# The fourth part of a modulation's weighted sums, moved from before the first latent head to beside it

## What is computed

```python
sh_m, sc_m, gt_m, sh_f, sc_f, gt_f = jnp.split(jax.nn.silu(c) @ w_ada + b_ada, 6, axis=-1)
h_lat = x * (1.0 + sc_m) + sh_m
q, k, v, log_decay_fwd, log_decay_bwd, g, p, bg = split(h_lat @ w_in)      # 4 heads
o = gla(q, k, v, log_decay_fwd, s_fwd) + flip(gla(flip(q), ...))           # chunks of 64 tokens
y = (sigmoid(bg_gla) * gla_output(o, g) + sigmoid(bg_pool) * pool(p)) @ w_out
x = layer_norm(ALPHA * x + gt_m * y)
x = layer_norm(ALPHA * x + gt_f * swiglu(x * (1.0 + sc_f) + sh_f))
```

## Time and profile before

| | us |
|---|---|
| median of three executions | 3194.3 |
| lowest, highest | 3191.63, 3194.87 |
| the profiled execution: its own time | 3199.43 |
| the profiled execution: span of the trace | 3197.8 |
| TensorE busy | 3015.1 (94%) |
| VectorE busy | 2197.3 (69%) |
| ScalarE busy | 1458.5 (46%) |

### The profile page before, as it was taken

The page is one execution under the profiler, slowest core; times in us unless marked ns, Lnnn a source line. Parts: engine busy times, 40 slices in busy tenths (PEclk is TensorE's granted clock), DMA queues, the critical chain, the costliest instruction groups (busy, mean ns, idle before and its releaser), DMA issues.

```text
span 3197.8 us, 40247 instructions
## 1 busy us (share of the span) xinstructions
PE 3015.1 (94%) x16596; PEld 2565.2 (80%) x16596; DVE 2197.3 (69%) x2696; ACT 1458.5 (46%) x1927; POOL 8.5 (0%) x21
## 2 busy tenths in 40 slices
PE   8989898999999999989949999999998999999997
PEld 7877787888888888866837787888876888888886
DVE  6455766899898977655566666658867776555556
ACT  5434655544444445444413444544443444444444
POOL 0000000000000000000000000000000000000000
PEclk9989998999999999999979999999998999999998
DMA  6535233677777875444573554568643775555552
GB/s 252 196 132 186 104 136 125 231 260 264 254 263 257 314 268 193 170 152 152 203 282 122 183 184 162 215 223 315 234 174 138 277 271 185 193 187 190 192 185 92
DMA packets 106517, 648.60 MB, mean 203 GB/s; under 512 B 11840, under 2 KB 11840, under 8 KB 42208
## 3 DMA queue, kind: packets, MB, share of 16 engines
q1 hardware_dynamic: 99792, 621.86, 54.2%
q10 hardware_dynamic: 4608, 16.78, 1.4%
q0 software_dynamic: 1936, 7.41, 0.6%
HBM read 635.51 MB, written 10.49 MB: 202 GB/s over the span
## 4 chain that ended last, share of the span: by engine, by line
PE 73%; DVE 15%; ACT 5%; issue 3%; DMA 3%; ACTq 0%; SPq 0%; DVEq 0%
PE PS L482 39%; PE PS L483 20%; DVE RL L1908 5%; DVE G L2325 3%; PE PS L520 3%; PE PS L521 3%; PE PS L522 3%; DMA G<-in_w_ada 2%; ACT RH L1151 2%; PE PS L1010 1%; PE PS L922 1%; PE PS L720 1%; DVE G L1967 1%; ACT G L1340 1%; DVE X L2246 0%
## 5 line engine op out<-in xcount | busy, mean ns | idle before, releaser
L482 PE MATMUL PS<-A,RH 128*128 128x512 f32 x4544 | 1629.3, 402 | 44.0 <-DVE A L2846 15.7
L1908 DVE TENSOR_TENSOR RL<-RW,RH 128x1024 fp32r<-128x1024 f32 x974 | 1177.4, 1222 | 630.8 <-ACT RH L1151 627.3
L1151 ACT ACTIVATE RH<-RW 128x1024 fp32r<-128x1024 f32 x974 | 1013.2, 1054 | 750.0 <-PE PS L483 599.0
L483 PE MATMUL PS<-A,RL 128*128 128x256 f32 x4544 | 1280.8, 282 | 0.0
L482 PEld LDWEIGHTS PS<-A,RH 128*128 128x128 f32 x4544 | 864.4, 190 | 257.6 <-issue 36.5
L483 PEld LDWEIGHTS PS<-A,RL 128*128 128x128 f32 x4544 | 869.3, 191 | 3.1 <-issue 2.6
L482 PE MATMUL PS<-H,RH 128*128 128x512 f32 x2304 | 812.6, 395 | 5.3 <-DVE RL L1908 5.2
L483 PE MATMUL PS<-H,RL 128*128 128x256 f32 x2304 | 643.1, 279 | 0.0
L482 PEld LDWEIGHTS PS<-H,RH 128*128 128x128 f32 x2304 | 431.7, 187 | 110.7 <-DVE RL L1908 4.2
L483 PEld LDWEIGHTS PS<-H,RL 128*128 128x128 f32 x2304 | 431.9, 187 | 0.3
L1156 ACT ACTIVATE LT<-PS 128x512 f32<-128x512 f32 x234 | 139.0, 594 | 329.2 <-PE PS L483 329.2
(11 more groups left out here) (259 smaller groups left out, 1660.3 us busy)
## 6 DMA issues: line engine op xcount, KB each, us to landing
RW<-in_w_fin SPq DMA_DIRECT2D x88, 1024.0 KB, 4.8
G<-in_w_ada SPq DMA_DIRECT2D x160, 512.0 KB, 5.9
RW<-in_w_up SPq DMA_DIRECT2D x64, 1024.0 KB, 4.9
RW<-in_w_down SPq DMA_DIRECT2D x64, 1024.0 KB, 5.1
RW<-in_w_fout SPq DMA_DIRECT2D x44, 1024.0 KB, 4.8
RW<-in_w_v SPq DMA_DIRECT2D x32, 1024.0 KB, 4.9
RW<-in_w_bg SPq DMA_DIRECT2D x32, 1024.0 KB, 4.9
RW<-in_w_k SPq DMA_DIRECT2D x16, 1024.0 KB, 4.8
```

Source lines behind the costliest of these rows:

```text
L482: t.matmul(bank[:, :], wh[:, k, cols], x, start=first and k == 0, stop=False, skip_group_check=True)
L483: done = t.matmul(bank[:, 0:256], wl[:, k, cols], x[:, 0, :], start=False, stop=last and k == 3, skip_group_check=True)
L1151: a.activation(m.high(x), m.slot(j)[:, x % 2 * HC:x % 2 * HC + HC], ACT.Copy).then_inc(s["hi"], 1)
L1908: v.tensor_tensor(m.low(x), m.slot(j)[:, x % 2 * HC:x % 2 * HC + HC], m.high(x).bitcast(F32), ALU.subtract).then_inc(s["lo"], 1)
```

## The change

`exhaust(beside)` goes away, and the lane of the modulation's sums is passed on to the heads' `run`, so that the items that are left are taken one by one between the steps of the first head. Their pace goes from 1.2 to 1.25 rounds per item.

```diff
-    beside = L.ada((4,), (1.2,))
+    beside = L.ada((4,), (1.25,))
     run(L.first_decay(), L.alpha_x(), L.k2(1), beside=beside)
     L.heads_begin()
     run(L.v2(), beside=beside)
-    exhaust(beside)
     for h in range(4):
-        run(slow(L.lat_head(h), 1.0 if h == 3 else 1.42), chain(idle() if h == 3 else L.v2(), L.bg2()))
+        run(slow(L.lat_head(h), 1.0 if h == 3 else 1.42), chain(idle() if h == 3 else L.v2(), L.bg2()), beside=beside)
```

## The result

The changed kernel takes 3175.73 us (median of four executions, 3175.31 to 3177.4) against 3192.97 us before (four executions, 3189.67 to 3194.87): the ratio is 0.994, with a 95% interval of 0.9923 to 0.9956, so 14 to 25 us are saved. Forecast were 30 us, 3164, with a range from 3149 to 3176. The time lies in the range, 0.3 us from its upper end, and the gain is a little over half of the one forecast.

A forecast was written before the change was run, and what follows sets the result against it. TensorE bounds the kernel, except for a hole before head 0 while VectorE finishes the modulation's sums. Of 48.2 us, 35.8 remain after VectorE's lateness; less 3, 1 and 1.6 for waits and clock, 30 us: 3164, range 3149 to 3176.

The forecast's parts named there:

- (a): Hole from the end of the `v2`'s last matmul to line 902 of head 0: 46.8 us removed.
- (b): After the hole TensorE runs at half clock: 1.0 us on line 902 and 2.2 on the next matmuls removed.
- the transposes: The 16 transposes come back inside head 0 on TensorE, adding 1.8 us: 50.0 - 1.8 = 48.2 saved if unhindered.
- VectorE's queue as the term that decides: Head 0's queries and keys stand behind the items in VectorE's in-order queue, holding TensorE at line 1010 of both directions.
- The start: VectorE begins head 0 (line 2567) at about 1650.5, 10.0 us after TensorE would; ends 1641 and 1654.
- First direction: Head 0, line 2567 to end of line 2600: 16.5 + 7.2 + 3.0 us on VectorE; TensorE held 11.9 us.
- Second direction: Head 0, to the second line 2600: 31.4 us on VectorE, line 1010 at 1708.6, 35.8 us saved without further waits.
- further waits: VectorE's waits in head 0: 3 us for loads (range 0 to 10), 1 for ScalarE (range 0 to 3).
- rival E: TensorE's short waits keep it at 1.2 GHz through head 0: 20 us slower, 3214; chance 0.03.
- A: The forecast: VectorE, late by its queue, holds TensorE twice in head 0; 20 to 40 us saved; chance 0.66.
- C: The two places feed too slowly, every item waits some 2.0 us; 9 to 20 us saved, 3185; chance 0.14.
- B: The items hide nearly completely beside head 0: 45 us saved, up to 48, 3149; chance 0.14.

The follow-up runs named there:

- e3_entry_free: Changed kernel with the last 16 items of the sums not loaded and worked on 1 column instead of 1024; 3145.66 us, ratio 0.9847.
- the early versions: Changed kernel with sums begun beside the first context head: without pause 3165.53 us, with 7 rounds left out 3148.64, that with early state load 3152.68.
- e2_pace_only: Kernel before with the new pace, 1.25 rounds per item, and the exhaust in its old place; 3195.5 us, ratio 0.9997.
- e2_move_only: Changed kernel with the old pace, 1.2 rounds per item; 3174.15 us, ratio 0.9934.
- e1_neither: Changed kernel with the 12 items beside head 0 not loaded and worked on 1 column instead of 1024; 3158.7 us, ratio 0.9884.
- e1_state_early: Changed kernel with head 0's carried state loaded some 70 us earlier, beside k2; 3172.54 us, ratio 0.993.
- the first set: First four experiments on the changed kernel: twelve items' work and loads removed, work removed, loads removed, or state loaded early; 3158.7, 3170.0, 3166.54, 3172.54 us.
- e1_loads_only: Changed kernel with all 32 loads, but VectorE working on 1 column instead of 1024 of the 12 items beside head 0; 3166.54 us, ratio 0.9901.
- e3_early_skip: Changed kernel with sums begun beside the first context head, 2.25 rounds per item, 7 rounds left out during token modulation; 3148.64 us, ratio 0.9855.

## Why the prediction was right or wrong, point by point

- **What bounds the kernel, and the hole**: right. It is gone from the slices, and e3_entry_free and the early versions, whose parts are 159.1 to 155.0 us, show that it was worth the 48 us that the terms (a), (b) and the transposes gave: 207.0 - 48.2 = 158.8. By the medians e3_entry_free saves 48.4 us.
- **VectorE's queue as the term that decides**: right in kind. TensorE waited for VectorE alone: 13.9 us in the first direction, where 12 were forecast, and 4.93 in the second, where it was 1 to 6. 8.4 of the 13.9 us were for splits, the rest ahead of lines 996, 1000 and 1010. One sign failed: VectorE should have been busy for over nine tenths from its entry to the second `Q4`, and it was busy for 53.85 of 64.45 us, 84%. The prediction's "58.1 us, nothing to spare" held 3.0 us of waiting for ScalarE as load, and compared VectorE's time with itself; TensorE, not held, needed 55.8 us there (1665.3 - 1640.5 + 31.0). The queue is late by its work and by its own waits together.
- **The start, "the load of the item, not VectorE, sets this time, so the new pace of 1.25 changes it little"**: this step failed in its size. It gave 1650.5, which is 83.1 us into the part; measured is +86.9, so 3.8 us of the 5.7 us between forecast (30.2) and part (24.5) stand here, and the upper end that I kept, 1654 or +86.6, was just passed. That a load sets the time was right: the eighteenth item's load was issued at 1640.58, its item began at 1650.12 after a wait of 3.84 us, and the twentieth waited 2.02. It is not because TensorE no longer stands still: in e2_pace_only it stands still from +71.9 on, with the old `exhaust` behind it, and the items are as late as in the change. There the eighteenth begins at +79.9 (now +80.1) and the twentieth at +85.8 (now +85.7):

```profile
1641.33 1.28 DVE L2325 SCALAR_TENSOR_TENSOR G<-G,SILT 128x1024 f32<-128x1024 f32 x1 [4.02 <-DMA G<-in_w_ada]
1642.54 1.22 DVE L1908 TENSOR_TENSOR RL<-RW,RH 128x1024 fp32r<-128x1024 f32 x1
1643.67 1.28 DVE L2325 SCALAR_TENSOR_TENSOR G<-G,SILT 128x1024 f32<-128x1024 f32 x1
1647.27 1.28 DVE L2325 SCALAR_TENSOR_TENSOR G<-G,SILT 128x1024 f32<-128x1024 f32 x1 [2.32 <-DMA G<-in_w_ada]
```

So the move does not delay them, and "the new pace of 1.25 changes it little" is the part of the sentence in doubt: all profiles at 1.25 with the state load in its place have the twentieth item at +85.7 to +87.0. But at 1.2 it stood at +81.9 before and at +86.1 in e2_move_only, so one execution's loads can do as much, and what made the 3.8 us stays open. That a microsecond at the entry is about one of the result holds for the whole of it: from e1_neither to e3_entry_free the entry moves by 12.3 us and the part by 11.3. For the 0.8 us of e1_state_early it did not show.
- **First direction**: 26.7 us forecast from line 2567 to the end of line 2600, 27.2 measured. Right, with 0.68 of it a wait for a load. The wait for ScalarE, 2.99 us, was the same to the hundredth.
- **Second direction**: 31.4 us of work forecast, 30.67 measured, but 37.3 us passed where 35.4 were forecast with the waits. The further waits were 3.00 us for ScalarE behind line 2567 (I took 1 of the range 0 to 3: the term was mis-sized), 1.62 for ScalarE's split, for which the sum had no term, and 1.54 for a load. The waits for loads in the head were 2.2 us against the 3 taken.
- **A place that was not seen**: TensorE's last and second longest wait in head 0, 4.93 us, was not for line 2600 or 2593 but for line 2345. The scores take the bank of PSUM in which the transposed sums still stand until VectorE has added them up, and that stands in its queue behind two splits and the second direction's far products. It cost little by itself: line 2600 ended at 1721.50 and line 1010 began at 1722.15, so without this wait it could have begun 0.65 us earlier at most.
- **The clock**: the first direction was granted 0.81 and the second 0.93, between the two levels of 1.2 and 2.4 GHz; rival E did not come about, and each fall followed a wait: behind the 6.30 us wait the first matmul took 0.79 us instead of 0.39.
- **The loads on SyncE, costed at nothing**: right for head 0, where ScalarE never waits for a weight chunk. Ahead of it ScalarE waits for one once, for 2.20 us, and TensorE's waits there are 2.2 us in all against 2.7 before.
- **The sum**: line 1010 of the second direction comes 24.8 us earlier in the part than before (+152.1 against +176.9), where 30.2 was forecast. Of the 5.4 us, 3.8 are the entry, 0.5 the first direction, 1.9 the waits of the second, less some of the clock's term. The 24.5 us in the part are not the 17.2 of the medians, though they lie in the interval of 14 to 25. The span outside of the part was 2990.8 us in the profile of before and 2993.2 in that of the change, and 2984.7 to 2992.3 in those of the first set. The profile of before was 5.1 us slower than its median. If that had stood in the hole, the gain forecast from it would have been too large by as much; but e2_pace_only, profiled in an execution of 3190.65 us, has a hole no shorter (part 209.9) and a span outside of only 2979.1. What the rest is stays open.
- **The rivals**: A's mechanism is what the traces show, but not its size: 17.2 us by the medians is below the 20 at its lower end and within C's 9 to 20. The range reached to 3176 only by the share kept for C, whose mechanism did not come about (2.2 us of waits for loads in the head, where C wanted over 15). That the time fell within it is in part luck. C was set aside with "the head's pace of 4.8 us per item", and that holds in the trace of the change. In that of e1_loads_only, without the items' work, the waits for loads in the head are 10.1 us; what they cost is 10.5 us by the part and 7.8, not clear of noise, by the medians. B's time of 3149 us was reached by two kernels once VectorE entered in step, but neither has all the items beside the head: e3_early_skip has them elsewhere, and e3_entry_free leaves out 16. The advice of the Trainium skill to interleave stretches with different busiest engines (Perfetto Trace Analysis, "Optimization Strategy") gave 14 to 25 us of the 48 here, and 45 where the items went beside the context heads. Occupancy did not tell the two apart: VectorE was busy for 53.41 of 84.10 us in head 1, 64%, and for 116.96 of 198.86 us from the first context head to k2, 59%.

## What to carry to other kernels

Work that is moved beside a full engine is not free when it stands in the queue of an engine that the full one follows step by step: count the busy time of that queue and its own waits from one meeting point to the next, not over the stage, and ask how late the queue is when the stage begins: here each was about half of the loss. An item that waits for a load inside an in-order queue holds all that stands behind it, and with two places a late load also delays the one after next: take its landing from loads in the same company (3.6 to 9.5 us in this one profile), with the upper end as well. If neither fits, look for a stretch further away with slack between the meeting points, and leave out the few rounds in which the two engines work in lockstep.

## What the runs showed of the hardware

A load of 512 KB took from 3.8 to 6.8 us to land beside the products before, and 4.4 in the median in the hole. At the head's start of the change one took 9.5 us (issued at 1640.58, its item began at 1650.12 after a wait of 3.84 us), when the state's 1 MB, which landed after 8.4 us, and two weight chunks, which took 9.0 and 8.9, were under way on two queues. With the state's load 70 us earlier (e1_state_early) the same load took 7.3 us. The clock fell from 2.4 to 1.2 GHz behind waits shorter than the hole: behind the one of the earlier trace rows, 2.68 us long, in the kernel before (granted 0.50 from 1630 to 1632), and in the change behind two of 1.57 and 2.91 us with 0.65 us of matmuls between them (granted 0.56 from 1678.0 to 1681.5).
